# Expert weight tiles: every second one on ScalarE's DMA queue, and eight places up to the 176th

## Time and profile before

| | us |
|---|---|
| median of 3 runs | 3623.2 (3623.05, 3623.2, 3630.44) |
| the profiled execution | 3625.26 |
| its span, first to last instruction | 3623.5 |
| TensorE busy in the span | 3399.2 (94%) |
| VectorE / ScalarE / GpSimd busy | 1448.7 / 702.8 / 192.5 |
| share of the 16 DMA engines for the queue of the loads | 41.0% |

### The profile page before, as it was taken

One profiled execution on the slowest core, in us unless ns is written; L12 is line 12 of the kernel. 1 busy time (PEld: TensorE's weight loads), 2 busy tenths in 40 slices (PEclk: granted clock), 3 DMA queues, 4 the chain that ended last, 5 costly groups with the idle time before them and its releaser, 6 DMA issues. The chain is left out here.

```text
span 3623.5 us, 56787 instructions
## 1 busy us (share of the span) xinstructions
PE 3399.2 (94%) x24513; PEld 2416.1 (67%) x24513; DVE 1448.7 (40%) x3086; ACT 702.8 (19%) x1553; POOL 192.5 (5%) x261
## 2 busy tenths in 40 slices
PE   8999999998888888889998999999999999999998
PEld 5877888433332333257777777788888888888666
DVE  2466455211011101123655455655532646544344
ACT  2127310200000000012454114212200101101232
POOL 0000000000000000000355000300000000000000
PEclk9999999999999999999999999999999999999999
DMA  6540114699999999970000220222222321221120
GB/s 243 194 154 22 48 71 186 271 428 428 428 428 426 424 425 426 423 287 24 3 4 16 78 73 27 95 72 78 86 89 74 100 87 48 92 82 62 49 71 24
DMA packets 130296, 602.01 MB, mean 166 GB/s; under 512 B 8288, under 2 KB 38752, under 8 KB 103552
## 3 DMA queue, kind: packets, MB, share of 16 engines
q1 hardware_dynamic: 125600, 589.94, 41.0%
q10 hardware_dynamic: 4448, 8.44, 1.0%
HBM read 587.82 MB, written 2.10 MB: 163 GB/s over the span
## 5 line engine op out<-in xcount | busy, mean ns | idle before, releaser
L3088 PE MATMUL banks<-slabs,ring 128*128 128x256 f32 (+1 forms) x4456 | 1002.1, 383 | 10.7 <-DVE ring L3234 4.1
L3088 PEld LDWEIGHTS banks<-slabs,ring 128*128 128x128 f32 x4456 | 841.9, 190 | 148.0 <-issue 24.5
L2337 PE MATMUL banks<-ring,slabs 128*64 128x512 f32 x2176 | 489.3, 598 | 76.1 <-DMA ring<-in_w_exp 69.5
L2337 PEld LDWEIGHTS banks<-ring,slabs 128*64 128x64 f32 x2176 | 154.6, 137 | 391.1 <-issue 304.5
L3088 PE MATMUL banks<-ring 128*128 128x256 f32 (+1 forms) x920 | 215.1, 382 | 4.1 <-DVE ring L3229 3.4
L2508 DVE TENSOR_TENSOR work<-work,banks 128x512 f32<-128x512 f32 x32 | 22.0, 687 | 488.2 <-PE banks L2337 470.2
L401 PE MATMUL banks<-slabs,ring 128*128 128x264 f32 (+3 forms) x712 | 196.0, 432 | 3.1 <-PEq L331 1.9
L3088 PEld LDWEIGHTS banks<-ring 128*128 128x128 f32 x920 | 173.2, 190 | 32.9 <-issue 8.6
L2337 PE MATMUL banks<-slabs 128*64 128x512 f32 x768 | 171.3, 595 | 17.7 <-DMA slabs<-in_w_exp 14.7
L3436 PE MATMUL banks<-slabs,ring 128*128 128x264 f32 x768 | 172.4, 386 | 1.6 <-issue 1.6
L401 PEld LDWEIGHTS banks<-slabs,ring 128*128 128x128 f32 (+1 forms) x712 | 132.1, 189 | 58.6 <-issue 35.3
(11 more groups left out here) (635 smaller groups left out, 4421.7 us busy)
## 6 DMA issues: line engine op xcount, KB each, us to landing
ring<-in_w_exp SPq DMA_DIRECT2D x144, 2048.0 KB, 15.8
slabs<-in_w_exp SPq DMA_DIRECT2D x48, 2048.0 KB, 32.6
ring<-in_w_in SPq DMA_DIRECT2D x19, 2048.0 KB, 11.7
ring<-in_w_ff SPq DMA_DIRECT2D x16, 2048.0 KB, 8.2
ring<-in_even_w_in SPq DMA_DIRECT2D x14, 2048.0 KB, 8.6
ring<-in_w_ada SPq DMA_DIRECT2D x12, 2048.0 KB, 10.5
ring<-in_w_out SPq DMA_DIRECT2D x4, 2048.0 KB, 8.4
ring<-in_even_w_out SPq DMA_DIRECT2D x4, 2048.0 KB, 8.5
```

The lines of the kernel that those rows point to most:

```text
L2337: ins = mm(out[64 * c:64 * c + CAP, :], lhsT[:, k, :], w[:, at:at + 512], start=first and k == 0, stop=last and k == 3)
L3088: last = mm(bank, a[:, k, :], b[:, k, :], start=k == 0, stop=k == h - 1)
```

## The change

1. There is one tensor for the four ring places and a connected stretch of slabs 3 to 6 for the four others (`places`). The small tensors of the stage move from slab 3 to slab 1, and the squares of the router from slab 3's to slab 1's region (`H`). The place order of tiles 8 and later is 4, 5, 6, 7, 0, 1, 2, 3.
2. Eight places are used up to tile 175 (`WIDE_RING = 22 * 8`), then the four of the ring.
3. Of tiles 8 to 175 the odd ones (84 tiles) are issued from ScalarE's own queue, at three points of each expert in its program: after `silu(e, 0)` those whose place was last that of a tile below 12e+2, after `silu(e, 1)` below 12e+6, and at the end of the expert below 12e+10. SyncE's queue skips these tiles.
4. In DRAM two consecutive tiles lie interleaved: partition p's 16 KB of the even tile, its 16 KB of the odd one, then partition p+1's.
5. SyncE waits for `pa`'s last pair on VectorE (which reads slab 3) before it loads tile 0.

```diff
-MORE_SLOTS, WIDE_RING = (6, 4, 5, 1), 8 * EXPERT_TILES
+MORE_SLOTS, MORE_FROM, WIDE_RING = 4, 3, 22 * 8
...
+    def places(self, slot, n):
+
+        size = KC * SLOT_COLS
+        if slot < SLOTS:
+            return self.in_ring[:, slot * size:(slot + n) * size]
+        at = MORE_FROM * self.slab_cols + (slot - SLOTS) * size
+        return self.slabs[:, at:at + n * size]
...
     def lay_slots(self, expert_tiles):
 
-        slots, first = SLOTS + len(MORE_SLOTS), expert_tiles[0]
+        slots, first = SLOTS + MORE_SLOTS, expert_tiles[0]
         freed = [*range(SLOTS, slots), *((first + i) % (SLOTS - 1) for i in range(SLOTS - 1)), SLOTS - 1]
...
-            slot = (freed[at % slots] if at < WIDE_RING else at % SLOTS) if n in expert_tiles else n if n < SLOTS else n % (SLOTS - 1)
+            in_turn = freed if at < slots else [*range(SLOTS, slots), *range(SLOTS)]
+            slot = (in_turn[at % slots] if at < WIDE_RING else at % SLOTS) if n in expert_tiles else n if n < SLOTS else n % (SLOTS - 1)
...
+            if n in expert_tiles and slots <= at < WIDE_RING and at % 2:
+                self.of_scalar.append(n)
...
     def issue_weights(self, engine, upto):
...
+            if n in self.of_scalar:
+                self.issued += 1
+                continue
...
+    def issue_from_scalar(self, act, used):
+
+        while self.of_scalar and self.before[self.of_scalar[0]] < used:
+            n = self.of_scalar.pop(0)
+            act.wait_ge(self.weight_used.sem, self.before[n] + 1)
+            self.nc.scalar.dma_start(self.ring_tile(n), self.tiles[n][0]).then_inc(self.weight_in[self.slot[n]].sem, 16)
...
-    squares = S3[:, :, 0:SEQ]
+    squares = H[:, :, 0:SEQ]
...
             sp.wait_ge(core.weight_used.sem, layer.last_tile + 1)
+            if layer is pa:
+                pa.pair_done(sp, 3)
...
-    xe = [flat[3][:, D * i:D * i + D].rearrange("p (k s) -> p k s", k=KC) for i in range(2)]
-    hT = flat[3][:, 2 * D:3 * D].rearrange("p (f s) -> p f s", s=CAP)
-    y = flat[3][:, 3 * D:4 * D]
+    xe = [flat[1][:, D * i:D * i + D].rearrange("p (k s) -> p k s", k=KC) for i in range(2)]
+    hT = flat[1][:, 2 * D:3 * D].rearrange("p (f s) -> p f s", s=CAP)
+    y = flat[1][:, 3 * D:4 * D]
...
                 silu(e, 0)
+                core.issue_from_scalar(act, tile(e, 2))
...
                 silu(e, 1)
+                core.issue_from_scalar(act, tile(e, 6))
                 keep_turned(e, 0)
...
                 if e != EXPERTS - 2:
                     keep_turned(e, 1)
+                core.issue_from_scalar(act, tile(e, 10))
...
-            core.tiles.append((dram["w_exp"][n].rearrange("p (k c) -> p k c", k=KC), KC, SLOT_COLS))
+            core.tiles.append((dram["w_exp"][n // 2].rearrange("p (i k c) -> p i k c", i=2, k=KC)[:, n % 2], KC, SLOT_COLS))
...
-    return tiles
+    return np.ascontiguousarray(tiles.reshape(-1, 2, P, 4 * D).transpose(0, 2, 1, 3)).reshape(-1, P, 8 * D)
```

More of the change, by code:

```diff
@@ L170, in __init__ @@
         sb = lambda name, shape, dt=F32: ctx.enter_context(nc.sbuf_tensor(name, shape, dt))
-        self.ring = [sb(f"ring{i}", [P, KC, SLOT_COLS]) for i in range(SLOTS)]
+        self.in_ring = sb("ring", [P, SLOTS * KC * SLOT_COLS])
         self.slab_cols = KC * TOK2
@@ L227, in __init__ @@
         self.deep = named(("product", "first", "second", "third", "fourth", "sums", "read", "step"), 20)
-        self.weight_in = [count(f"weight_in_slot{i}") for i in range(SLOTS)] + turn[37 - len(MORE_SLOTS):]
-        self.ring += [self.slab[i][:, 0:KC * SLOT_COLS].rearrange("p (k c) -> p k c", k=KC) for i in MORE_SLOTS]
+        self.weight_in = [count(f"weight_in_slot{i}") for i in range(SLOTS)] + turn[37 - MORE_SLOTS:]
+        self.ring = [self.places(i, 1).rearrange("p (k c) -> p k c", k=KC) for i in range(SLOTS + MORE_SLOTS)]
         self.weight_used = count("weight_used")
@@ L287, in plan_laid_out @@
         self.tiles.append((w[i].rearrange("p (k c) -> p k c", k=KC), KC, SLOT_COLS))
+    def places(self, slot, n):
[4 more added lines that the diff above has]
+        return self.slabs[:, at:at + n * size]
     def lay_slots(self, expert_tiles):
-        slots, first = SLOTS + len(MORE_SLOTS), expert_tiles[0]
+        slots, first = SLOTS + MORE_SLOTS, expert_tiles[0]
         freed = [*range(SLOTS, slots), *((first + i) % (SLOTS - 1) for i in range(SLOTS - 1)), SLOTS - 1]
-        self.slot, self.turn, self.before, last, turns = [], [], [], {}, [0] * slots
+        self.slot, self.landing, self.before, last, self.landings = [], [], [], {}, [0] * slots
+        self.of_scalar = []
         for n in range(len(self.tiles)):
             at = n - expert_tiles[0]
-            slot = (freed[at % slots] if at < WIDE_RING else at % SLOTS) if n in expert_tiles else n if n < SLOTS else n % (SLOTS - 1)
+            in_turn = freed if at < slots else [*range(SLOTS, slots), *range(SLOTS)]
+            slot = (in_turn[at % slots] if at < WIDE_RING else at % SLOTS) if n in expert_tiles else n if n < SLOTS else n % (SLOTS - 1)
             self.slot.append(slot)
-            self.turn.append(turns[slot])
             self.before.append(last.get(slot))
             last[slot] = n
-            turns[slot] += 1
+            if n in expert_tiles and slots <= at < WIDE_RING and at % 2:
+                self.of_scalar.append(n)
+            self.landings[slot] += 1
+            self.landing.append((slot, self.landings[slot]))
     def issue_weights(self, engine, upto):
@@ L325, in weight_ready @@
     def weight_ready(self, engine, n):
-        landed = self.weight_in[self.slot[n]]
-        engine.wait_ge(landed.sem, landed.at(16 * (self.turn[n] + 1)))
+        slot, turn = self.landing[n]
+        landed = self.weight_in[slot]
+        engine.wait_ge(landed.sem, landed.at(16 * turn))
     @contextmanager
@@ L2234, in experts @@
     for landed, slot in zip(core.weight_in[SLOTS:], range(SLOTS, len(core.weight_in))):
-        landed.add(16 * core.slot.count(slot))
+        landed.add(16 * core.landings[slot])
     core.weight_limit = core.rwkv_limit
```

## The result

The changed kernel takes 3635.3 us (median of 7 runs, 3630.0 to 3640.1), the kernel before 3624.4 us in the same comparison (7 runs, 3623.1 to 3632.1). The ratio is 1.0027, with a 95% interval of 1.0018 to 1.0037: slower by 0.27%, some 10 us. The forecast was no change.

The account below looks back on a forecast made before the run. The prediction took the expert stage's stream of loads, with DMA engines never free, as the bound. Terms -2.3 + 2.4 + 0 = +0.1 us gave 3625.4 us profiled and a forecast median of 3623 us, range 3608 to 3645.

Parts of the forecast that it names:

- Bound: Expert stage: it lasts as long as its stream of loads; a microsecond of idle DMA engines moves the end by one.
- Eight places for 80 tiles more: Tiles 96 to 175: the longer queue raises 425 GB/s to 427 or 428, -2.3 us, bounds 0 and -5.5.
- The gap at the start: Near 693 us: tiles 11 and 12 are issued later, leaving a gap in the loads of +2.4 us, bounds 0 and +4.
- 84 issues on ScalarE: ScalarE in the expert stage: 28 to 52 us of issuing, hidden by its waits for TensorE, 0 us.
- The rate of two queues: 168 expert tiles: 427 to 428 GB/s as with one queue, 0 us; bounds 413, far 385, and 436 GB/s: +30, +92, -15 us.
- Sharing of the engines: Expert loads: two move at once and land in pairs; new waits stay inside TensorE's 84 us, no queue empties, 0 us.
- the last 16 tiles and the tail behind the last landing are as before: End of the expert stage and what follows it: claimed unchanged.
- The sum: Whole kernel: -2.3 + 2.4 + 0 = +0.1 us; profiled execution 3625.4 us, runs' median 3623.
- The signs for the next profile: Expert stage: 427 to 428 GB/s, dip near 693 us, landings over 30 us, some 85 us of waits, last landing near 1585.
- the odd queue runs dry: Rival, expert stage: ScalarE's points come late; 1 us idle at each of 42 groups of four, +42 us minus depth's gain; chance 0.06.
- streams that disturb each other: Rival, expert loads: two streams on one engine lower the rate; 422 GB/s gives +12 us, 3635; 413 gives 3653; chance 0.15.
- the likeliest case's own range: Whole kernel: the range of the forecast of no change itself, 3617 to 3629 us.

Follow-up runs that it names:

- the three kernels with no gap that counts: Changed kernel with every expert tile on SyncE, step at 176 or 184, or ScalarE issuing only odd tiles 17 to 159, step at 184: 3622.7, 3625.1, 3623.6 us.
- all on SyncE: Changed kernel with every expert tile issued from SyncE's queue; places, DRAM order and step at tile 176 kept: 3622.7 us, ratio 0.9994.
- ScalarE to 159: Changed kernel with ScalarE issuing odd tiles only up to 159, SyncE all from 160 on, step at 176 kept: 3624.7 us, ratio 1.0000.
- ScalarE from 17: Changed kernel with ScalarE issuing odd tiles only from 17 on; 9, 11, 13 and 15 go from SyncE: 3629.1 us, ratio 1.0012.
- six points: Changed kernel with three more points in ScalarE's program at which it issues odd tiles: 3627.2 us, ratio 1.0011.
- the kernel with tiles 17 to 159: Changed kernel with ScalarE issuing only the 72 odd tiles 17 to 159 and the step to four places at tile 184: 3623.6 us, ratio 0.9996.
- the kernel without the dip: Changed kernel with every expert tile on SyncE's queue and the step to four places at tile 184: 3625.1 us, ratio 1.0000.
- the kernel without the first point: Changed kernel without the first of ScalarE's three issue points, the one after silu(e, 0): 3719.7 us, ratio 1.0262 (4 runs).

## Why the prediction was wrong, point by point

- **Bound.** Right for the landings: the stage's length follows them in every run, down to 914 us, and the three kernels with no gap that counts have 914.0, 914.0 and 914.3 us. That "a microsecond of idle DMA engines, or one saved, moves the end by one" is wrong where the idle time is taken from the mean share: with all on SyncE 1.5 us are missing from the share at the step, and no tile lands later.
- **Eight places for 80 tiles more, -2.3 us.** Right in sign, too large. All-on-SyncE, which has this and all other edits but the queue, is 1.0 us shorter than before. The rise from 425 to 427 or 428 GB/s is there, but most of it is a dip in the mean that the landing of tiles doesn't feel: from the landing of tile 96 to that of tile 178 it takes 405.4 us before and 404.5 with all on SyncE. The term measures -0.9 us, within its bounds.
- **The gap at the start, +2.4 us.** Right in place and size: a share of 0.67 and 0.53 at 692 to 696 us, and 916.5 - 914.0 = 2.5 us between the two kernels that differ by it and the tiles up to 159. In the changed kernel itself tile 175 lands 836.9 us after the start of tile 0, against 834.5 with all on SyncE: 2.4 us.
- **84 issues on ScalarE, 0.** Right. From 740 to 1440 us they take 0.33 us in the median and 1.02 at most, and at the start the copy behind `silu(e, 1)` came at 695.04 us in time.
- **The rate of two queues, 0.** Right: 427 to 428 GB/s from 740 us to 1440 us in the changed kernel and in all experiments but the last, whichever queue issues. The far bounds, 385 and 436 GB/s, were never approached. The Trainium skill's rule that loads from several issuing engines run on the same 16 DMA engines (DMA: Bandwidth & Descriptors, "Issuing engines are not separate DMA queues") agrees with this rate.
- **Sharing of the engines, 0**, and with it "the last 16 tiles and the tail behind the last landing are as before". **This is the step that failed.** I asked whether a queue can empty in the steady stretch, and there it can't. I didn't ask it at the one place where the loads must stop for lack of places: the step from eight to four at tile 176, in front of which TensorE does a combine. Tile 176 can be issued when TensorE has used 172, some 15.1 us after it got 171 (3.6 + 7.9 + 3.6). Its load then takes 8.5 to 8.7 us to land, and 4.9 of them are its turn in the stream. So it must go 3.7 us before the last load in flight lands, or the stream stops. The landings give both halves for each kernel:

| kernel | from 171's landing to 175's, us | 176 issued, against 175's landing | 176 lands later than in a stream by | cost of the step by the lengths, us |
|---|---|---|---|---|
| all on SyncE | 19.6 | 4.4 before | 0.0 | reference |
| ScalarE to 159 | 19.6 | 4.4 before | 0.0 | reference |
| ScalarE from 17 | 19.0 | 1.0 before | 2.6 | 2.8 |
| six points | 15.3 | 0.1 before | 3.7 | 3.6 |
| changed | 11.0 | 4.2 after | 7.9 | 7.7 |

  The last column is the difference from all-on-SyncE, and for the changed kernel, which has the gap at the start too, from ScalarE to 159. In order on one queue tiles 172 to 175 follow 171, and the step is covered. With two queues the even tiles have gone ahead in part by the time 171 lands, and in the changed kernel 172 is all there. Of the 7.7 us, 3.6 remain when the odd tiles are issued early (six points), and 4.1 go with ScalarE's late issues. ScalarE from 17 is the other way round: its odd tiles are ahead and TensorE waits for the even ones. It starts the combine 822.0 us after tile 0, against 829.5 in the changed kernel, and so leaves tile 172 early enough to lose less.
- **The sum.** -1.0 + 2.5 + 7.7 = +9.2 us closes by itself, since its terms are differences of the lengths of before, all-on-SyncE, ScalarE to 159 and changed. The landings are a check of their own: -1.0 for what all-on-SyncE gains, +2.4 at the start and +7.9 at the step give +9.3, against +9.2 measured.
- **The signs for the next profile.** The rate, the dip near 693 us and TensorE's 85 us of waiting (48.6 + 36.8) came as said. Landings of over 30 us for both queues did not: their medians from 740 to 1440 us are 23.5 and 27.2 us, and so the reserve was smaller than I took it for. The last expert load landed at 1596.6 us, not near 1585.
- **The rival "the odd queue runs dry"** had the mechanism (even tiles land first and stop at the tile that TensorE lacks) but at the wrong place: in 42 groups instead of at one step, for +42 us and with a chance of 0.06. Taken one point further it does come to that, 86 us. The other slower rival, streams that disturb each other, had its price (3635 us) near the result by accident; the rate shows nothing of it. It is also by luck that 3635 us lies inside the range of 3608 to 3645: its upper part was drawn for that rival, and the likeliest case's own range ended at 3629.

What stays open: the kernel with ScalarE from 17 shows that the issue of tiles 9 to 15 decides which queue gets ahead, but no run shows why the lead then lasts for 150 tiles.

## What to carry to other kernels

When a stream of loads sets the end, look at each place where the pool of buffers shrinks or the order of issue changes, and compare there the loads still in flight with the work that the consumer has before it frees the next buffer. The loads must last longer than that work by what a load needs from its issue to its landing beyond its turn in the stream, 3.7 us here. The steady stretch says nothing about it. A second queue for half of an ordered stream buys no bandwidth where one queue holds the engines at a share of 1.01, and it spends reserve: tiles come in pairs, and the later queue decides. If it is used, keep it away from the start and from such steps, as the kernel with tiles 17 to 159 does at no cost.

## What the runs showed of the hardware

- Two queues with 2048 KB loads outstanding had the rate of one: 428 GB/s from 740 to 1440 us with all on SyncE, and with two queues at three points or at six. In the changed kernel and in the one with ScalarE from 17 one queue was behind all that time: TensorE's matmuls waited 68 us for its tiles and for the other's not at all (with six points 64 and 4 us).
- A load of 2048 KB issued when the queues were empty or nearly so took 8.5 to 8.7 us from issue to landing (tile 176 in three kernels), while loads in a stream landed 4.9 us apart.
- The 16 parts of a landing drift apart. With all on SyncE they come over 1.9 us from tile 14 to 56, 3.5 us from tile 57, 5.0 from 107 and 6.6 from 157. At each of these three tiles, 50 apart, the last part comes 1.5 us late and the first does not; what happens there no run shows.
- A dip in the mean DMA share need not delay a landing. With all on SyncE the share was 0.59 for 3 us at the step, and the tiles behind it landed no later than in the kernel without the dip (849.3 and 849.2 us after tile 0). In the changed kernel the share went to 0.00 for 3 us, and the tiles did come later.
- A long wait of TensorE cost more than its length. In the kernel without the first point it waited 7.44 us for a tile, and the 16 matmuls after it took 6.53 us instead of 3.65:

```profile
900.00:905.00 5.00, 0.58 (x2) 0.30 (x4) 0.00 (x0) 0.00 (x0) 0.00 (x0) 0.50 1.01 433
905.00:910.00 5.00, 5.00 (x14) 1.42 (x12) 0.00 (x0) 0.00 (x0) 0.00 (x0) 0.50 0.99 426
910.00:915.00 5.00, 5.00 (x24) 1.54 (x22) 0.69 (x1) 0.00 (x0) 0.00 (x0) 0.98 1.00 429
```

TensorE's last matmul before the wait ended at 897.0 us. The granted clock is at its lower level, 1.2 GHz (0.50), from 900.0 to 910.2 us, so for the first 5.8 us of the matmuls too. Over the stretch from 740 to 1440 us the clock is 0.92 there, against 1.00 with all on SyncE. With ScalarE at tiles 17 to 159 it is 0.97, and this costs nothing, since the loads set the pace: 914.3 us against 914.0.
